# Latent attention in a fused two-block fp32 kernel: probabilities turned on VectorE and by DMA instead of on TensorE

## The reference, cut to what matters

```python
def causal_block_attention(q, k, v):
    ...
        sc = jnp.einsum('bqhd,bkhd->bhqk', qblk.astype(jnp.float32), kf) * scale
        sc = jnp.where(kpos[None, :] <= qpos[:, None], sc, -jnp.inf)
        p = jax.nn.softmax(sc, axis=-1)
        return jnp.einsum('bhqk,bkhd->bqhd', p, vf)
    ...
def token_mixer(...):
    ...
    h_ml = mlstm_chunkwise(q_ml, k_ml, v_ml, i_pre, f_pre)
    h_ml = rmsnorm(h_ml, ml_head_norm) * jax.nn.sigmoid(o_ml)
    h_mla = causal_block_attention(q, k, kv[..., MLA_NOPE:])
    return jnp.concatenate([h_ml, h_mla], axis=-1) @ w_out
```

## Time and profile before

| | |
|---|---|
| median of 3 runs | 1533.84 us (1533.41 to 1534.88) |
| the profiled execution | 1533.96 us, span 1532.2 us |
| TensorE busy | 1506.4 us, 98% of the span |
| VectorE, ScalarE, GpSimd busy | 73%, 49%, 41% of the span |
| granted TensorE clock | 0.999 of full speed |
| a chunk: load, cast, remainder | lands 3.6 us after its issue (median); 1.05 us; 2.48 us (means) |
| a pair's 512 columns: cast to mix_hi, mix_lo | 0.58 us, 0.69 us |

### The profile page before, as it was taken

One profiled execution on the slowest core, in us unless ns is written; L12 is line 12 of the kernel. 1 busy time (PEld: TensorE's weight loads), 2 busy tenths in 40 slices (PEclk: granted clock), 3 DMA queues, 4 the chain that ended last, 5 costly groups with the idle time before them and its releaser, 6 DMA issues.

```text
span 1532.2 us, 20428 instructions
## 1 busy us (share of the span) xinstructions
PE 1506.4 (98%) x7106; PEld 1244.1 (81%) x7106; DVE 1122.7 (73%) x1860; ACT 749.1 (49%) x1259; POOL 627.4 (41%) x280
## 2 busy tenths in 40 slices
PE   9999999999999999999999999999999999999998
PEld 7888888888888877888888888767778888888887
DVE  5689999987875455777767769777745897667774
ACT  6553333454552445755544236454763745444444
POOL 3454444433344432343344635341534244444451
PEclk9999999999999999999999999999999999999999
DMA  5333332355443323333333133222103433333321
GB/s 209 97 124 96 96 96 96 96 168 154 147 151 98 97 80 110 103 104 110 107 98 98 49 93 95 88 70 70 35 22 103 145 110 97 96 98 110 98 95 56
DMA packets 46179, 155.74 MB, mean 102 GB/s; under 512 B 5124, under 2 KB 9348, under 8 KB 45832
## 3 DMA queue, kind: packets, MB, share of 16 engines
q1 hardware_dynamic: 45072, 150.95, 31.1%
q10 hardware_dynamic: 1016, 3.61, 0.7%
HBM read 147.20 MB, written 7.35 MB: 101 GB/s over the span
## 4 chain that ended last, share of the span: by engine, by line
PE 85%; DVE 7%; issue 3%; ACT 3%; DMA 1%; POOL 1%; SPq 0%; DVEq 0%; ACTq 0%; POOLq 0%
PE bank L709 83%; DVE bias L2380 1%; DMA w_raw<-in_stream 1%; DVE x_sq L2298 0%; DMA dn_raw<-in_stream 0%; PE bank L1312 0%; DVE cq_rstd L2234 0%; ACT w_hi L1535 0%; POOL res L678 0%; ACT dn_first L1829 0%; POOL w_lo L581 0%; ACT relu L1671 0%; PE bank L1128 0%; PE bank L1485 0%; DVE cn_lo L2941 0%
## 5 line engine op out<-in xcount | busy, mean ns | idle before, releaser
L581 POOL TENSOR_TENSOR w_lo<-w_raw,w_hi 128x1024 fp32r<-128x1024 f32 x191 | 471.8, 2481 | 513.4 <-ACT w_hi L1535 513.1
L709 PE MATMUL bank<-a_hi,w_hi 128*128 128x512 f32 (+1 forms) x1120 | 444.9, 397 | 1.8 <-DVE a_lo L3200 1.4
L709 PE MATMUL bank<-a_hi,w_lo 128*128 128x512 f32 (+1 forms) x1120 | 431.4, 385 | 0.0
L709 PE MATMUL bank<-a_lo,w_hi 128*128 128x512 f32 (+1 forms) x1120 | 431.1, 385 | 0.0
L1535 ACT CAST w_hi<-w_raw 128x1024 fp32r<-128x1024 f32 x199 | 204.7, 1047 | 182.6 <-DMA w_raw<-in_stream 182.5
L709 PEld LDWEIGHTS bank<-a_hi,w_hi 128*128 128x128 f32 x1120 | 210.5, 188 | 48.2 <-issue 3.9
L709 PEld LDWEIGHTS bank<-a_lo,w_hi 128*128 128x128 f32 x1120 | 210.6, 188 | 45.4 <-issue 3.4
L709 PEld LDWEIGHTS bank<-a_hi,w_lo 128*128 128x128 f32 x1120 | 210.4, 188 | 42.5
L593 POOL TENSOR_TENSOR dn_rest<-dn_raw,dn_second 128x1024 fp32r<-128x1024 f32 x39 | 93.7, 2433 | 249.5 <-DVE dn_rest L2673 249.5
L709 PE MATMUL bank<-dn_rest,f_hi 128*128 128x512 f32 x364 | 141.7, 389 | 0.0
L1829 ACT CAST dn_first<-dn_raw 128x1024 fp32r<-128x1024 f32 x54 | 55.6, 1048 | 157.8 <-DVE dn_raw L2654 157.8
(11 more groups left out here) (434 smaller groups left out, 2797.2 us busy)
## 6 DMA issues: line engine op xcount, KB each, us to landing
w_raw<-in_stream SPq DMA_DIRECT2D x199, 512.0 KB, 3.6
dn_raw<-in_stream SPq DMA_DIRECT2D x56, 512.0 KB, 3.6
p_parts<-d_parts SPq DMA_DIRECT2D x8, 640.0 KB, 4.0
d_turned<-p_parts SPq DMA_DIRECT2D x32, 160.0 KB, 3.4
res<-in_xT ACTq DMA_DIRECT2D x1, 2048.0 KB, 9.7
out_y<-res_tok SPq DMA_DIRECT2D x8, 256.0 KB, 2.0
x_raw<-in_xT SPq DMA_DIRECT2D x3, 512.0 KB, 8.8
mem_raw<-in_memT SPq DMA_DIRECT2D x1, 1024.0 KB, 12.4
```

The lines of the kernel that those rows point to most:

```text
L581: nc.gpsimd.tensor_tensor(w_lo[:, j, :], w_raw[:, j, :], w_hi[:, j, :].bitcast(F32), ALU.subtract).then_inc(w_lo_done, 1)
L709: return nc.tensor.matmul(o, l, r, start=start, stop=stop)
```

## The change

Each head's probabilities are now normalised in place by ScalarE (`l_probs`, with the inverse sum as scale), turned in 32x32 squares by VectorE into `l_parts`, stored to DRAM by SyncE in two parts (the first three query blocks, then the fourth), and read back into `l_turned` in four pieces. TensorE's transposes, the copies of L2064, `o_rows` and the pair turns are gone. The values of head h are ten products with the values of a pair of heads as the stationary side and 128 query columns as the moving side, at step 4h + 7; their result already has features on partitions, and the half that belongs to head h is cast and subtracted (`latent_hi`, `latent_lo`). VectorE's transpose of block n stands in step n + 1 behind the recurrent scores. Score banks rotate over three instead of two. ScalarE's casts of seven chunks come up to six steps later, GpSimd's remainders and `ml_lo` wait for the recurrent diagonals (`behind_diagonals`), SyncE's chunk loads stand between the stores and reads. Six units of the third projection block stand ahead of the values of head 7. The first value unit does not wait for the gate's eviction. At the end of the kernel the outputs of the third token block stand ahead of the last three sums.

```diff
+        l_probs = [at(f"l_probs{qb}", [P, (qb + 1) * P], o)
+                   for qb, o in enumerate((B0 + 32768, TMP0 + 11264, G0 + 30848, TMP0 + 9216))]
+        l_parts = at("l_parts", [P, RING, TRIANGLE, PART], TMP0 + 4096)
+        l_turned = at("l_turned", [P, RING, TRIANGLE, PART], B0)
...
+            def latent_out(h, done, k):
+                sp.wait_ge(sems["pT_ready"], 4 * (MLA_G + h) + done)
+                sp.wait_ge(sems["p_stored"], 16 * (HEADS + 2 * h + done - 3))
+                sp.dma_start(p_parts[HEADS + h].rearrange("p (g k j) -> p g k j", g=RING, k=TRIANGLE)[:, :, k, :],
+                             l_parts[:, :, k, :]).then_inc(sems["p_stored"], 16)
+
+            def latent_back(h):
+                sp.wait_ge(sems["p_stored"], 16 * (HEADS + 2 * h + 2))
+                if h == 0:
+                    sp.wait_ge(sems["gates_turned"], 1)
+                else:
+                    sp.wait_ge(sems["pv_done"], 4 * MLA_G + h)
+                rows_back(HEADS + h, l_turned)
+
+            rings_at = {6: CH["OA"] + 5, 7: CH["OA"] + 6, 10: CH["OA"] + 7, 12: CH["WO"], 15: CH["WO"] + 1,
+                        21: CH["WO"] + 2, 27: CH["WO"] + 3}
+            for n in range(4 * MLA_HEADS):
+                if n % 4 == 2:
+                    latent_out(n // 4, 3, slice(0, part_of(3, 0)))
+                if n % 4 == 3:
+                    latent_out(n // 4, 4, slice(part_of(3, 0), TRIANGLE))
+                    latent_back(n // 4)
+                if n in rings_at:
+                    ring(rings_at[n])
...
+            def behind_diagonals(heads):
+                pool.wait_ge(sems["ml_diag"], TB * heads)
+
+            remainder(CH["OM"], CH["OM"] % RING)
+            behind_diagonals(2)
+            remainder(CH["OM"] + 1, (CH["OM"] + 1) % RING)
             for unit in (15, 16, 17, 18):
                 second_residual(unit, residual_steps[unit])
+            behind_diagonals(3)
+            remainder(CH["OM"] + 2, (CH["OM"] + 2) % RING)
             ml_lo(0)
+            remainder(CH["WO"], 0)
             remainder(CH["WO"] + 1, 1)
             for unit in (23, 24, 25, 26):
                 second_residual(unit, residual_steps[unit])
+            behind_diagonals(4)
             ml_lo(1)
             remainder(CH["WO"] + 2, 2)
             ml_lo(2)
+            pool.wait_ge(sems["ml_var"], ML_HEADS)
             remainder(CH["WO"] + 3, 3)
...
-                if k == 0:
+                if k == 0 and tb > 0:
                     pe.wait_ge(evac_dve, o - DVE_FROM)
...
             def latent_scores(n):
-                pe.wait_ge(sems["p_ready"], U0 + n - 1)
-                mla_score(MLA_G + n // 4, n % 4, ps[4 + n % 2][:, 0:(n % 4 + 1) * P]).then_inc(sems["s_ready"], 1)
-
-            def latent_turn(n):
-                pe.wait_ge(sems["p_ready"], U0 + n + 1)
-                pe.wait_ge(sems["pT_copied"], 4 * XH + n)
-                for kb in range(n % 4 + 1):
-                    r = slice(kb * P, (kb + 1) * P)
-                    m = nc.tensor.transpose(ps[6][:, r], probs[:, n % 2, r], ident)
-                m.then_inc(sems["pT_ready"], 1)
-
-            def latent_values(n):
-                h, nk = n // 4, n % 4 + 1
-                pe.wait_ge(sems["pT_copied"], 4 * XH + n + 1)
-                if n % 8 == 0:
-                    pe.wait_ge(sems["o_ready"], MLA_G + n // 8)
-                else:
-                    pe.wait_ge(sems["o_scaled"], n)
-                for kb in range(nk):
-                    m = mm(ps[2][:, 0:MLA_V], probsT[:, n % 2, kb * P:(kb + 1) * P],
-                           v_mla[kb // 2][:, kb % 2, h * MLA_V:(h + 1) * MLA_V], kb == 0, kb == nk - 1)
+                if n >= 3:
+                    pe.wait_ge(sems["p_ready"], U0 + n - 2)
+                mla_score(MLA_G + n // 4, n % 4, ps[4 + n % 3][:, 0:(n % 4 + 1) * P]).then_inc(sems["s_ready"], 1)
+
+            def latent_values(h):
+                pe.wait_ge(sems["p_landed"], 16 * RING * (HEADS + h + 1))
+                pe.wait_ge(sems["o_ready"], MLA_G + h)
+                pair = slice(P * (h // 2), P * (h // 2) + P)
+                for qb in range(TB):
+                    for kb in range(qb + 1):
+                        m = mm(ps[2][:, qb * P:(qb + 1) * P].rearrange("p (g j) -> p g j", g=RING),
+                               v_mla[kb // 2][:, kb % 2, pair], l_turned[:, :, part_of(qb, kb), :], kb == 0, kb == qb)
                 m.then_inc(sems["pv_done"], 1)
-
-            def pair_turn(p):
-                pe.wait_ge(sems["o_scaled"], 8 * p + 8)
-                for qb in range(TB):
-                    m = nc.tensor.transpose(ps[2][:, qb * P:(qb + 1) * P], o_rows[p][:, qb, :], ident)
-                m.then_inc(sems["o_turned"], 1)
...
             for n in range(4 * MLA_HEADS):
                 if n + 2 < 4 * MLA_HEADS:
                     latent_scores(n + 2)
-                turning = n >= 8 and n % 8 == 1
-                if n >= 8 and n % 8 == 2:
-                    latent_values(n - 2)
                 ml_hook(n)
-                if turning:
-                    pair_turn(n // 8 - 1)
-                latent_turn(n)
-                if n >= 1 and not turning:
-                    latent_values(n - 1)
+                if n % 4 == 3 and n >= 7:
+                    latent_values(n // 4 - 1)
                 ml_turns(n)
-            latent_values(4 * MLA_HEADS - 1)
-            pair_turn(MLA_HEADS // 2 - 1)
...
+            for i in range(6):
+                wo_step(2, i)
+            latent_values(MLA_HEADS - 1)
             for j in range(WO_WHOLE):
-                for i in range(6 if j < 2 else 0, KB):
+                for i in range(6 if j < 3 else 0, KB):
...
-            cast_at = {8: CH["VM"] + 1, 9: CH["VM"] + 2, 10: CH["VM"] + 3, 11: CH["OM"], 16: CH["OM"] + 1, 22: CH["OM"] + 2, 28: CH["WO"]}
+            cast_at = {9: CH["VM"] + 1, 12: CH["VM"] + 2, 15: CH["VM"] + 3, 17: CH["OM"], 19: CH["OM"] + 1,
+                       24: CH["OM"] + 2, 30: CH["WO"]}
...
-                act.wait_ge(sems["pT_ready"], U0 + n - 1)
-                act.wait_ge(sems["p_inv"], U0 + n - 1)
-                r = slice(0, (n % 4 + 1) * P)
-                A.activation(probs[:, n % 2, r], ps[4 + n % 2][:, r], ACT.Exp, bias=negmax[:, n % 2:n % 2 + 1],
-                             scale=-1.0, accum_out=rowsum[:, n % 2:n % 2 + 1]).then_inc(sems["p_ready"], 1)
-
-            def latent_turned(n):
-                act.wait_ge(sems["pT_ready"], U0 + n + 1)
-                act.wait_ge(sems["pv_done"], U0 + n - 1)
-                r = slice(0, (n % 4 + 1) * P)
-                A.copy(probsT[:, n % 2, r], ps[6][:, r]).then_inc(sems["pT_copied"], 1)
-
-            def pair_hi(p):
-                act.wait_ge(sems["o_turned"], p + 1)
-                A.copy(mix_hi[ML_HEADS + p], ps[2][:, :]).then_inc(sems["o_hi"], 1)
+                if n >= 8:
+                    act.wait_ge(sems["p_inv"], U0 + n - 7)
+                if n >= 4:
+                    act.wait_ge(sems["pT_ready"], U0 + n - 3)
+                A.activation(l_probs[n % 4][:, :], ps[4 + n % 3][:, 0:(n % 4 + 1) * P], ACT.Exp,
+                             bias=negmax[:, n % 2:n % 2 + 1], scale=-1.0, accum_out=rowsum[:, n % 8:n % 8 + 1]
+                             ).then_inc(sems["p_ready"], 1)
+
+            def latent_scaled(n):
+                act.wait_ge(sems["p_inv"], U0 + n + 1)
+                A.activation(l_probs[n % 4][:, :], l_probs[n % 4][:, :], ACT.Copy, scale=rowinv[:, n % 8:n % 8 + 1]
+                             ).then_inc(sems["p_scaled"], 1)
+
+            def latent_hi(h):
+                r = slice(MLA_V * (h % 2), MLA_V * (h % 2) + MLA_V)
+                act.wait_ge(sems["pv_done"], U0 + h + 1)
+                A.copy(mix_hi[ML_HEADS + h // 2][r, :], ps[2][r, :]).then_inc(sems["o_hi"], 1)
...
+            def latent_turn(n):
+                qb = n % 4
+                dve.wait_ge(sems["p_scaled"], U0 + n + 1)
+                if n >= 4 and qb in (0, 3):
+                    dve.wait_ge(sems["p_stored"], 16 * (HEADS + 2 * (n // 4) - (qb == 0)))
+                V.transpose(l_parts[:, :, part_of(qb, 0):part_of(qb, qb) + 1, :].rearrange("p g k j -> p k g j"),
+                            l_probs[qb].rearrange("p (k g i) -> p k g i", g=RING, i=PART)
+                            ).then_inc(sems["pT_ready"], 1)
...
-                turning = n >= 8 and n % 8 == 1
-                if n >= 8 and n % 8 == 2:
-                    latent_scaled(n - 2)
-                if turning:
-                    pair_lo(n // 8 - 1)
                 ml_first(n)
-                if n >= 1 and not turning:
-                    latent_scaled(n - 1)
+                if n >= 1:
+                    latent_turn(n - 1)
+                if n % 4 == 0 and n >= 8:
+                    latent_lo(n // 4 - 2)
                 ml_rest(n)
-            latent_scaled(4 * MLA_HEADS - 1)
-            pair_lo(MLA_HEADS // 2 - 1)
+            latent_turn(4 * MLA_HEADS - 1)
```

(15 more changed lines are left out.)

75 lines of the change are left out of this document (40 added, 35 removed).

## The result

The changed kernel takes 1542.78 us (median of 4 runs, 1542.07 to 1542.87), the kernel before, timed beside it, 1533.62: a ratio of 1.0055 with a 95% interval of 1.0043 to 1.0067. It is 9 us slower where the prediction said 6 us faster. The profiled execution took 1542.75 us, its span is 1540.9 (before: 1532.2), and its mean granted clock is 0.994 of full speed (0.999).

The account below looks back on a forecast made before the run. TensorE, busy 98% of the span, was taken to bound the kernel. Start -3.5, four-step stretches -6.1, end +4.4 and tail -0.8 sum to -6.0 us: 1528.0 from 1533.96, given as 1527.8, range 1520 to 1535.

Parts of the forecast that it names:

- L = 7.0: From transpose's end to values: store 2.6, issues 1.3, last read 3.1, 7.0 us in all; ends 5.9 and about 9.5.
- T of head 3: In the stretch from step 16, the fourth block's transpose ends 3.4 us into the step.
- TensorE's own work: In the changed stage, 26.5 us of transposes, value products and turns leave, 17.6 come: 8.9 us less.
- max(W, T + L) + 2.2: Length of a four-step stretch: the larger of TensorE's work W and transpose end plus trip, then 2.2 us of values.
- the turn's predicted wait: After step 28, the last recurrent head's turn waits 1.3 us, its squares behind ScalarE's cast of WO+3.
- I cost this at nothing: VectorE's +9.4 us and ScalarE's +7 stay far below TensorE and add nothing on the path, except in the last stretch.
- The start: Up to step 4: the gate's 1.1 us wait goes, chunk VM+3's remainder limits next; -3.5 us.
- The end: From step 28: 21.9 us for 21.2, then head 7's values, 2.2, and a bare wait of 1.5; +4.4 us.
- The tail: At the kernel's end, outputs ahead of block 6's sum bring the last sum to 1525.9 instead of 1526.7: -0.8 us.
- The slower case: Rival: the trip decides; at 9.5 us it makes the kernel +7, 1541 us; slower by over 3 from 8.8; chance 0.09.
- only eats the gain: Rival: a trip of 8.2 us, or VectorE's transposes stretched under GpSimd's passes, leaves 1534 us; chance 0.15.
- the prediction's own case: Four or five landing waits, together 7 to 12 us, giving 1525 to 1530.5 us; chance 0.51.

Follow-up runs that it names:

- e10: Changed kernel, values of heads 0 to 6 later, head 7's earlier, fourth-block transposes first, OM cast earlier, plus two edits (WO+3 loaded earlier, cast later): 1519.60 us, ratio 0.9913.
- e3: Changed kernel with ScalarE's cast for OM one entry earlier and SyncE's load of WO+3 between head 6's two stores: 1543.65 us, ratio 1.0061.
- e7: Changed kernel with VectorE transposing each head's fourth block ahead of the recurrent work, not behind it: 1531.72 us, ratio 0.9989.
- e11: Changed kernel with only ScalarE's cast of WO+3 moved behind the squares of the last recurrent head: 1542.83 us, ratio 1.0056.
- e1: Changed kernel with extra products that change nothing filling TensorE's idle time ahead of the values of heads 3, 5 and 6: 1536.91 us, ratio 1.0024.
- e8: Kernel before, with only the first value unit's wait for the gate's eviction removed: 1532.51 us, ratio 0.999.
- e12: e10 without GpSimd's waits for the recurrent diagonals and the last variance, same order of passes: 1523.29 us, ratio 0.9927.
- e6: Changed kernel without GpSimd's waits for the recurrent diagonals and the last variance, same order of passes: 1544.74 us, ratio 1.0067.

## Why the prediction was wrong, step by step

Three steps failed. The trip was given one length, L = 7.0, and took 8.2 on average. The sum had no term for TensorE's clock behind a wait, which cost about 5 us. And T of head 3 left out three products, 2.1 us. The rest of the sum came out to within 1.5 us a term.

**TensorE's own work: right.** Between the earlier trace rows and e10, both at a clock of 0.999, it falls by 10.8 us (predicted 8.9). (A thousandth of the clock is 1.5 us of busy time, so the 1.9 more are hardly a difference.) In the changed kernel only 4.2 us of it is seen, since the lower clock stretched the rest. VectorE gained 5.5 us (9.4 predicted), ScalarE 7.0 (7).

**The trip, L = 7.0: right in two heads, short in three.** From the transpose's end to the values it took 7.2 us in heads 3 and 5. It took 8.0 in head 4 (four issues in 2.43 us, the slow case of the earlier trace rows), 9.1 in head 6, whose slowest read landed in 5.2 us, with the load of WO+3 and the first store of head 7 issued right behind (4.3 us in e3, without that load), and 9.5 in head 1, landing in 5.7 beside ScalarE's 256 KB load of mrow. So two heads came near the upper end, and both had reads of over 4.5 us, which the prediction had named as a sign of being wrong. The estimate of 6.3 us from the Trainium skill (DMA: Bandwidth & Descriptors, Anatomy of one DMA) lies under every one of them, by 0.9 at the least; by its heading that section describes transfers that GpSimd issues, and these are SyncE's, so it should not have been applied as it stands. The first attention's rows were the better guide. The step that failed here is "little else is in the queue here": chunk loads stand right behind the reads of five heads, and the DMA share of the six four-step stretches is 0.29 to 0.65, against 0.07 to 0.36 in the earlier trace rows. A load behind the reads does not do it alone, since head 3 has one and took 7.2. For head 6, e3 shows 1.0 us of its 2.1 (8.1 us without the load); for head 1 no run moved the load of mrow, and the cause stays open.

**T, when the transpose ends: one term wrong.** 4.4, 2.0, 3.7, 2.0 and 2.7 us into the step in heads 1, 2, 4, 5 and 6 are as predicted. Head 3 took 5.5 for 3.4: the term "then mask or product 0.3 to 0.7" left out the three products with tanh that ml_first issues in step 16, of which two were slow beside GpSimd.

**The formula max(W, T + L) + 2.2: right with the measured T and L as long as the clock holds, wrong when it falls.** Measured against predicted:

| stretch | predicted | after | e7 | what made the difference in the changed kernel |
|---|---|---|---|---|
| start, from the first latent score | 16.2 | 16.8 | 16.8 | |
| from step 4 | 17.4 | 18.8 | 18.2 | 0.9 for v_ml |
| step 8 | 13.6 | 16.4 | 14.0 | L 2.5, slow values 0.2 |
| step 12 | 13.3 | 13.0 | 13.0 | |
| step 16 | 12.6 | 16.4 | 12.9 | T 2.1, slow values 1.4 |
| step 20 | 12.9 | 14.1 | 13.0 | L 1.0 |
| step 24 | 11.6 | 13.5 | 12.0 | slow values 1.6 |
| step 28 and 12 units | 21.9 | 24.8 | | L 2.1, slow values 2.1, less 1.3 |

The less 1.3 is the turn's predicted wait, which did not come: it was hidden (e11). In the stretch from step 8 TensorE also waited 2.6 us for OM and ran OM's six products slowly, but T + L (4.4 + 9.5 us) ended at the same moment, as e1 and e3 show, so this is counted once. The prediction is nearly e7's column, but by luck: in e7 the transposes end earlier than the predicted T, the trips are longer than 7.0 (8.5 in head 3), and in the stretch from step 8 it is OM's wait of 2.1 us that decides. In all the stage's sum was short by 14 us: 5.6 by L, 5.3 by value products at the lower clock, a term that the sum did not have, 2.1 by T, 2.0 in the first two stretches, less the 1.3; small differences make up the rest.

**Chunk OM: wrong, without a price.** "I cost this at nothing" was argued for busy time; the cast (1062.1, before 1062.0) and GpSimd's 2.5 us behind it were not followed against a TensorE that arrives earlier. e3 shows that head 1's trip takes the place of this wait, so it added nothing in the changed kernel; in e7 it set the stretch, 0.4 us over the prediction.

**The start:** -2.9 for -3.5; the gate's wait is 0.95 by e8, and chunk VM+3's remainder ends at 1030.6 (1028.23 + 2.37), as by the earlier trace rows. **The end:** head 7's values and a bare wait of 1.4, predicted 1.5: right. **The tail:** -0.76 in the trace, predicted -0.8: right.

**The rivals.** The slower case had the right place and the right name, the trip, with 0.09; its price came from L alone, and its stated point, L of 8.8, was not reached on average (7.2 to 9.5 in heads 1, 3, 4, 5 and 6, mean 8.2). By the prediction's own price a mean of 8.2 only eats the gain, 1534; the way from there to 1542.8 is the clock, T of head 3 and the first two stretches. That the time lies near the 1541 given is luck. So is the near miss of the prediction's own case, four or five landing waits of 7 to 12 us together: there were four, of 12.3, but what followed them was not priced. VectorE: DVE Perf Modes (The three transpose paths, and Rules for kernel authors) in the Trainium skill spoke for it: full transposes to TensorE. The changed kernel sides with that rule; e10 does not: with the same detour, covered, it is 13 us faster than the kernel before, and only 1.7 us of that belong to the start (0.95, e8) and the tail (0.76). What decided was whether the trip was hidden.

What stays open: why the reads of heads 1 and 6 landed late beyond the 1.0 us of e3; which of e10's two edits counts; e12 and e6 do not settle the size of the second part's gain, and the 1.4 us more than predicted in the stretch from step 4 was not taken apart beyond v_ml.

## What to carry to other kernels

When a wait is traded for work on the bound engine, price the wait twice: the idle time, and the products behind it at the clock they will get. Put the start of a long trip first in its engine's step and its consumer as late as the buffers allow, and only then count what is saved; the same 32 transposes by transfer stand in a kernel 9 us slower and in one 13 us faster than the kernel before, by what stood around them. When the bound engine comes earlier, follow every chunk's load, cast and remainder again, and see that a chunk has landed when its cast comes up ahead of work that a chain needs.

## What the hardware showed that was not expected

The granted clock after a wait is not a function of that wait alone. Twenty value products took 2.40 us without one. Behind 2.32 us of idle time they took 4.01 in the changed kernel, behind 2.27 and 2.31 us in e7 they took 2.50, and behind 2.23 in e6 4.13; 3.3 to 5.2 us were followed by 3.83 to 4.64 every time. And a wait of 0.32 us in e6 was followed by 3.27, with a wait of 2.64 six products earlier, while in e1, behind the same 2.64 and then 1.08, they took 2.47. What decides between them these runs don't tell; a wait of over 3 us was never free.

Half-speed products are not the only way in which idle time spreads: an operation of VectorE beside a remainder of GpSimd took 2.76 us for 0.69, and one such pass in the wrong place delays a whole recurrent step by 2 us.
